# A two-layer streaming block in fp32 on TensorE: a new order for the steps between the q projections and the first merge, and form F7 made by VectorE

## The reference, cut to what matters

```python
h = rms_norm(x, norm_g)
proj = h @ w_in
(q, k, v, z_a, p_in, z_b, u, v_sgu, z_c, glu_a, glu_b, z_d, merge) = jnp.split(proj, SPLIT_POINTS, axis=-1)
q = apply_rope(rms_norm(q.reshape(B, S, N_Q_HEADS, HEAD_DIM), q_norm_g), cos, sin)
k = apply_rope(rms_norm(k.reshape(B, S, N_KV_HEADS, HEAD_DIM), k_norm_g), cos, sin)
o_a = window_attention(q, k, v, attn_sinks)
o_c = spatial_gating(u, v_sgu, sgu_ln_g, sgu_ln_b, sgu_w, sgu_b)
...
branches = jnp.stack([o_a * jax.nn.silu(z_a), o_b * jax.nn.silu(z_b), o_c * jax.nn.silu(z_c), o_d * jax.nn.silu(z_d)], axis=2)
branch_out = jnp.einsum('bsnw,nwd->bsnd', branches, w_branch)
gates = jax.nn.sigmoid(merge.reshape(B, S, N_BRANCHES, D))
return x + jnp.sum(gates * branch_out, axis=2) @ w_out
```

## Time and profile before

| | |
|---|---|
| Time, median of 3 runs | 2082.21 us (2080.82 to 2083.49) |
| Profiled execution, its own time | 2081.95 us |
| Its span, first to last instruction | 2080.2 us |
| Mean granted TensorE clock | 0.994 of full speed |
| Busy: TensorE | 2052.1 us, 99% |
| Busy: VectorE, GpSimd, ScalarE | 1359.6, 1307.6, 906.0 us (65, 63, 44%) |
| HBM | 88 GB/s over the span |
| Chain of work that ended last | TensorE 90%, VectorE 5% |

### The profile page before, as it was taken

The page is one execution under the profiler, slowest core; times in us unless marked ns, Lnnn a source line. Parts: engine busy times, 40 slices in busy tenths (PEclk is TensorE's granted clock), DMA queues, the critical chain, the costliest instruction groups (busy, mean ns, idle before and its releaser), DMA issues.

```text
span 2080.2 us, 27152 instructions
## 1 busy us (share of the span) xinstructions
PE 2052.1 (99%) x9592; PEld 1698.6 (82%) x9592; DVE 1359.6 (65%) x1601; ACT 906.0 (44%) x1679; POOL 1307.6 (63%) x984
## 2 busy tenths in 40 slices
PE   9899999999999999999998999999999999999999
PEld 8788777888888888888887887778888888888887
DVE  6967444688978645338779665447888786453384
ACT  6564565243233434324645546543332333343342
POOL 2666544776669776654738664447767696675545
PEclk9999999999999999999999999999999999999999
DMA  7022332413431343313421232323235313434132
GB/s 273 26 77 75 87 122 72 127 51 72 84 84 51 82 86 76 133 57 111 143 90 36 76 96 88 102 84 104 61 72 95 74 51 82 82 81 137 46 132 102
DMA packets 122214, 186.13 MB, mean 89 GB/s; under 512 B 30688, under 2 KB 39648, under 8 KB 122080
## 3 DMA queue, kind: packets, MB, share of 16 engines
q1 hardware_dynamic: 104496, 155.01, 24.1%
q0 software_dynamic: 9216, 16.78, 6.0%
q10 hardware_dynamic: 8368, 12.60, 1.8%
HBM read 141.34 MB, written 41.95 MB: 88 GB/s over the span
## 4 chain that ended last, share of the span: by engine, by line
PE 90%; DVE 5%; ACT 1%; POOL 1%; issue 1%; DVEq 1%; DMA 0%; SPq 0%; ACTq 0%; POOLq 0%
PE acc L786 81%; PE acc L843 2%; PE aux L843 2%; DVE flo L1601 2%; PE aux L955 1%; DVE x L1605 1%; PE aux L946 1%; PE aux L936 1%; PE aux L904 1%; PE aux L970 1%; POOL wsum L705 1%; DVE stv L1976 0%; PE acc L1010 0%; DMA raw<-wstream 0%; SPq L548 0%
## 5 line engine op out<-in xcount | busy, mean ns | idle before, releaser
L786 PE MATMUL acc<-fhi,whi 128*128 128x512 f32 x2136 | 840.9, 394 | 7.2 <-DVE v L1598 3.0
L786 PE MATMUL acc<-flo,whi 128*128 128x512 f32 x2136 | 835.8, 391 | 0.0
L786 PE MATMUL acc<-fhi,wlo 128*128 128x512 f32 x2136 | 835.6, 391 | 0.0
L701 POOL TENSOR_TENSOR wlo<-raw,whi 128x512 fp32r<-128x512 f32 x392 | 541.9, 1384 | 432.6 <-ACT whi L1062 431.7
L786 PEld LDWEIGHTS acc<-fhi,whi 128*128 128x128 f32 x2136 | 403.5, 189 | 96.9 <-issue 7.7
L786 PEld LDWEIGHTS acc<-fhi,wlo 128*128 128x128 f32 x2136 | 403.1, 189 | 84.3
L786 PEld LDWEIGHTS acc<-flo,whi 128*128 128x128 f32 x2136 | 403.5, 189 | 82.2
L701 POOL TENSOR_TENSOR wlo<-wsum,whi 128x512 fp32r<-128x512 f32 x222 | 315.6, 1422 | 235.3 <-ACT whi L1062 234.8
L1062 ACT ACTIVATE whi<-raw 128x512 fp32r<-128x512 f32 x392 | 244.6, 625 | 342.2 <-PE acc L786 301.1
L1605 DVE SCALAR_TENSOR_TENSOR aux<-conv,allp,aux 128x1024 f32<-128x1024 f32 x232 | 299.0, 1289 | 20.0 <-issue 0.4
L1062 ACT ACTIVATE whi<-wsum 128x512 fp32r<-128x512 f32 x222 | 139.3, 628 | 213.7 <-PE acc L786 139.5
(11 more groups left out here) (236 smaller groups left out, 2286.0 us busy)
## 6 DMA issues: line engine op xcount, KB each, us to landing
raw<-wstream SPq DMA_DIRECT2D x392, 256.0 KB, 2.7
md<-prev POOLq DMA_DIRECT2D x64, 256.0 KB, 4.3
x<-x SPq DMA_DIRECT2D x32, 256.0 KB, 5.2
md<-prev SPq DMA_DIRECT2D x32, 256.0 KB, 3.3
out<-x ACTq DMA_DIRECT2D x32, 256.0 KB, 2.1
mx<-md SPq DMA_DIRECT2D x24, 256.0 KB, 4.9
xrow<-x_rows SPq DMA_DIRECT2D x8, 512.0 KB, 6.8
qs<-qd SPq DMA_DIRECT2D x32, 128.0 KB, 2.7
```

The costliest lines, as they stand in the source:

```text
L701: nc.gpsimd.tensor_tensor(wlo[:, f % SLOTS, :], src, whi[:, f % SLOTS, :].bitcast(F32), ALU.subtract).then_inc(lo_made, 1)
L786: mm = nc.tensor.matmul(dst, w, m[:, kt0 + k, cols], start=first and k == 0 and n == 0, stop=last and k == UK - 1 and n == 2, skip_group_c ...
```

## The change

It does four things, in both layers:

1. **F7 on VectorE.** `form_7` and its semaphore go; `form` makes F7 between the rests of B22 and F6, with two subtractions more on VectorE, and ScalarE's rounding of F7 waits for `form_made`.
2. **Statistics.** VectorE's sixteen `bn_stats` move from between the rests of F5 and F7 to three places: two tiles behind F4, three behind F4's rest, three behind `square_low(L, 0)`. The aggregates, `sgu_var` and the rest of the scales then follow, so that they stand behind `sum_21` of Q0, which waits for Q0's p4. On ScalarE `sgu_scales` and `normal_vs(L, 0)` move from Q0's p3 and p4 to Q1's p6, and `normal_vs(L, 1)` from Q1's p2 to p4. F4's rounding moves behind the weight copy of p5.
3. **Head sums and mix.** On TensorE k's head sums move from ahead of p1 to ahead of p5 of Q1, the first mix from p2 to p3, q's first head sums from p4 of Q1 to ahead of U0. ScalarE's inverse roots, `square_high`, `swap_k` and `load_rope` move with them (`load_rope` from behind the copy of p7 to behind that of p3).
4. **Rotation.** In ZC0 VectorE's table and turn of q's second half move from behind `gate_rest` C22 to behind `sum_22`, and join from behind the whole pair to behind `gate_rest` C22.

```diff
-        MADE = [(q, n) for q in ("F5", "F6", "F4") for n in range(2)]
+        MADE = [(q, n) for q in ("F5", "F7", "F6", "F4") for n in range(2)]
...
-            def form_7(L):
-
-                pool.wait_ge(form_made, form_n(L, MADE, "F5", 1))
-                for n in range(2):
-                    at = slice(2 * n, 2 * n + 2)
-                    nc.gpsimd.tensor_tensor(x12[:, at, :], x22[:, at, :], x12[:, at, :], ALU.subtract).then_inc(f7_made, 1)
-
...
-                form_7(L)
                 row_low(L)
...
-                pair(L, "Q", 1, {"p1": lambda L=L: head_sums(L, 0), "p2": lambda L=L: sgu_mix(L, (0, 1)),
-                                 "p4": lambda L=L: head_sums(L, 1)})
-                pair(L, "U", 0)
+                pair(L, "Q", 1, {"p5": lambda L=L: head_sums(L, 0), "p3": lambda L=L: sgu_mix(L, (0, 1))})
+                pair(L, "U", 0, {"p1": lambda L=L: head_sums(L, 1)})
...
                 plain_pair("Q", 0, first_of(qlo[0]), {
-                    "p1": lambda: take_kv(L, 1), "p6": lambda: form_rounded(L, ("F4", 0), ("F4", 1)),
-                    "p2": lambda: (take_turned_k(L), square_a(L, 0), square_high(L, 0)),
-                    "p3": sgu_scales, "p4": lambda: normal_vs(L, 0, range(TT))})
+                    "p1": lambda: take_kv(L, 1), "p5": lambda: form_rounded(L, ("F4", 0), ("F4", 1)),
+                    "p2": lambda: (take_turned_k(L), square_a(L, 0), square_high(L, 0))})
                 plain_pair("Q", 1, first_of(qlo[1]), {
-                    "p1": lambda: (square_a(L, 1), square_b(L, 1), inverse_root(L, 0)),
-                    "p6": lambda: swap_k(L), "p5": lambda: square_high(L, 1),
-                    "p7": lambda: load_rope(L), "p2": lambda: normal_vs(L, 1, range(TT)),
-                    "p3": lambda: inverse_root(L, 1)})
-                plain_pair("U", 0, None, {"p6": lambda: square_a(L, 2), "p5": lambda: square_b(L, 2)})
+                    "p1": lambda: (square_a(L, 1), square_b(L, 1)),
+                    "p6": lambda: (sgu_scales(), normal_vs(L, 0, range(TT))),
+                    "p5": lambda: inverse_root(L, 0),
+                    "p7": lambda: (square_high(L, 1), swap_k(L)),
+                    "p3": lambda: load_rope(L), "p4": lambda: normal_vs(L, 1, range(TT))})
+                plain_pair("U", 0, None, {"p1": lambda: inverse_root(L, 1), "p6": lambda: square_a(L, 2),
+                                          "p5": lambda: square_b(L, 2)})
...
-                    if q == "F6":
-                        dve.wait_ge(f7_made, 2 * L + n + 1)
                     dve.drain()
                     if q == "F5":
                         op = sub(b11, b11, b12)
+                    elif q == "F7":
+                        op = sub(b12, b22, b12)
...
                 form_rest(L, ("B22", 0), ("B22", 1))
+                form(L, "F7")
                 form(L, "F6")
...
                 form_rest(L, ("F6", 0), ("F6", 1), ("F5", 0), ("F5", 1))
-                dve.wait_ge(vs_taken, 8 * L + 8)
-                gate_stats(range(TT))
                 form_rest(L, ("F7", 0), ("B21", 0), ("F7", 1), ("B21", 1))
                 form(L, "F4")
+                dve.wait_ge(vs_taken, 8 * L + 8)
+                gate_stats(range(2))
                 sum_x(L, "Q", 0)
                 sum_v(L, "Q", 0)
                 sum_22(L, "Q", 0, qhi[0][:, HALF:SEQ])
                 form_rest(L, ("F4", 0), ("F4", 1))
+                gate_stats(range(2, 5))
+                sum_12(L, "Q", 0, qlo[0][:, HALF:SEQ]).then_inc(taken["c"], 1)
+                sum_21(L, "Q", 0, qhi[0][:, 0:HALF]).then_inc(taken["d"], 1)
+                square_low(L, 0)
+                gate_stats(range(5, TT))
+                dve.drain()
                 for t in range(TT):
                     nc.vector.bn_aggr(mv[:, t, :], stv[:, t, :, :])
...
-                sum_12(L, "Q", 0, qlo[0][:, HALF:SEQ]).then_inc(taken["c"], 1)
-                square_low(L, 0)
+                row_bias()
+                sum_x(L, "Q", 1)
                 dve.wait_ge(sgu_root, L + 1)
...
-                sum_21(L, "Q", 0, qhi[0][:, 0:HALF]).then_inc(taken["d"], 1)
-                row_bias()
-
                 add_squares(L, 1)
-                sum_x(L, "Q", 1)
                 sum_v(L, "Q", 1)
+                sum_22(L, "Q", 1, qhi[1][:, HALF:SEQ])
                 square_low(L, 1)
-                sum_22(L, "Q", 1, qhi[1][:, HALF:SEQ])
...
-                gate_pair(L, "ZC", 0, branch_c, 0, 0, {"x": lambda: join(0), "11": lambda: (table(1), turn(1))})
-                join(1)
+                gate_pair(L, "ZC", 0, branch_c, 0, 0, {"x": lambda: join(0), "22": lambda: (table(1), turn(1)),
+                                                       "11": lambda: join(1)})
```

More of the change, by code:

```diff
@@ L326, in hybrid_block @@
         form_made = sem("form_made")
-        f7_made = sem("f7_made")
         form_hi = sem("form_hi")
@@ L1155, in form_rounded @@
                         act.wait_ge(h_scaled, 16 * L + {"B11": 0, "B22": 8, "B21": 12}[q] + 2 * (n + 1))
-                    elif q == "F7":
-                        act.wait_ge(f7_made, 2 * L + n + 1)
                     else:
```

## The result

The changed kernel takes 2063.34 us (median of four runs, 2063.27 to 2063.84); the kernel before, run beside it on the same chip, 2082.43 (2080.82 to 2083.49). The ratio is 0.991, with a 95% interval of 0.9892 to 0.9927: 19.1 us less, nearly twice the forecast 10.2, and 0.7 us under the lower end of the range. The profiled execution spans 2061.5 us against 2080.2, 18.7 less.

The account below looks back on a forecast made before the run. TensorE, busy 99% of the span, bounds the kernel, so only its waits and low clock can be won back: 30.1 us gone less 19.9 new, net 10.2, takes 2081.95 to 2071.8 us; range 2064 to 2079.

Parts of the forecast that it names:

- the gate mix: Ahead of p3 of Q1, both layers: new TensorE wait of 5.6 us plus 3.0 of low clock, 17.2 in all.
- the rotary tables: Loaded later behind the mix, delaying k's rotation: TensorE waits 1.1 us per layer at U0's p4, 2.2 in all.
- Gone, 30.1: Old TensorE waits and low clock removed: head sums 14.1, form 4.5, probabilities 10.1, small ones 1.4 us.
- The probabilities: Waits for normalised probabilities, both layers, go as q's stores and the weight unit behind them come earlier: 10.1 us.
- The head sums' cause: k's squares in Q1 late because ScalarE rounded F4 ahead of p4's copy, which GpSimd's sums awaited; 14.1 us goes.
- S: Start of Q1's p1, when Q0's p4 ends and sum_21 can run; the mix's chain was counted to S + 20.1.
- The 3.0: Low clock charged behind each gate mix wait, in us; bounds 1.7 and 3.4.
- v1, 0.5: First layer: v1 from 1.3 us before to 1.3 after TensorE's p3 asks; 0.5 us charged.
- The mix in time: Rival at the gate mix: no wait, only 3 of the 20 us come, some 2054 to 2056; chance 0.08.
- the probabilities did not wait: Rival at the probabilities: they still wait, 4 to 10 of 10.5 us missing, 2076 to 2082; chance 0.18.
- idle lap of GpSimd: Slower rival: a lap of 4 to 6 us ahead of ScalarE's sqrt delays mix and head sums; chance 0.06.
- the signs that the forecast named: In the new profile: mix waits 5 to 7 us, clock 0.5 to 0.6 behind, 1 us at U0's p4, old waits gone.

Follow-up runs that it names:

- the run alone: Only the second q rotation moved ahead of ZC0's first gates, on the kernel before: 2069.43 us, ratio 0.9944.
- the run with the root first: Kernel after, with k's inverse root on ScalarE ahead of the gate's normalised halves, right behind the sqrt: 2057.27 us, ratio 0.9881.
- the last run: Kernel after with root first, mix one product later, q's six rotation products behind v1's bank work, plus four statistics back between rests of F5 and F7: 2052.08 us.
- rounding moved: Kernel before, with ScalarE's copy for p4 of Q0 put ahead of its rounding of F4: 2079.71 us, ratio 0.9991.
- form alone: Kernel before, with only form F7 moved from GpSimd to VectorE, the sixteen statistics left in place: 2079.58 us, ratio 0.9992.

## Why the prediction was wrong in size and right in kind

All the old waits went, and the one new wait of some length came where the forecast had it. Two terms of the sum failed: the gate mix, charged 17.2 us and measured 12.9, and the rotary tables, charged 2.2 and measured nothing. What the sum called gone was also some 3 us too small; the ledger gives the places of that, and only in part its causes. Point by point, by its own terms.

- **Gone, 30.1.** All of it went. **The probabilities** were forecast at 10.1, or 10.5 with GpSimd's 0.45. The ledger has 11.0 at this place in the changed kernel and in the run alone: waits of 6.7, GpSimd's 0.45 in the second layer, 3.4 of lower clock (7.2 x 0.24 behind each wait), and 0.5 that no wait shows. So this term was about right. The medians' 12.3 alone and 11.9 on top have intervals over 2 us to either side, and the run alone had also less of the lower clock behind the head sums (below), which is no merit of the rotation. **The head sums' cause** was only partly as stated: the rounding made a third to a half of their lateness.
- **New: the mix, 17.2; measured 12.9.** This is the step that failed most. The waits are 5.04 and 4.08, not 5.6 each, which is 2.1 of the 4.3 us; the lower clock is the other 2.2. The chain had two errors that in the first layer partly cancel: the variance came 1.4 us later (sum_21 starts at S + 1.1 instead of 0.3, and the aggregates and the two products with rms take 0.4 longer than charged), and reciprocal to shift took 0.7 instead of 2.5, because its two 128x8 products took 0.96 and 1.16 us in the trace of before only beside GpSimd's pieces; now GpSimd's last piece ends at 106.2, and they take 0.17 each. In the second layer sum_21 starts at S + 0.3 as forecast, the normalisations at S + 9.3, and the wait is 1.0 shorter. The lower clock cost 2.1 and 1.7 where I took 3.0 each. The 3.0 came from the waits of 3.5 and 4.6 in one execution. In the run of the rotation alone the same waits, 3.57 and 4.55 us, are followed by only half of it:

```profile
103.80:111.00 7.20, 7.14 (x24) 5.73 (x25) 3.98 (x9) 4.76 (x10) 3.62 (x3) 0.76 0.24 73
1131.40:1138.60 7.20, 7.17 (x24) 5.75 (x25) 3.95 (x8) 4.79 (x10) 3.59 (x3) 0.76 0.29 73
```

  7.2 x 0.24 = 1.7 in each, against 2.9 and 3.1 in the earlier trace rows. The mix's own price differs as well: with the rotation back, waits of 5.05 and 4.09 us are followed by 7.2 us at 0.65 and 0.66, 2.5 and 2.4 us lost. I had taken a value that differs from one execution to the next for a constant.
- **New: rotary tables, 2.2; measured nothing.** Their issue is as late as forecast, 3.2 us behind the mix's end (125.76; before 0.5), but they land 4.4 us later instead of 7.2: k's rotation starts 1.4 us behind U0's start, forecast 3.9. Its first product took 2.18 us (before 1.28). The two products behind `xs` took 1.23 us each, where the trace of before shows 1.90 and 2.16 beside GpSimd's pieces. Issue by ScalarE's queue, then VectorE:

```profile
125.76 0.44 ACTq L1259 DMA_DIRECT2D sint<-rope  x1
...
130.21 2.18 DVE L1594 SCALAR_TENSOR_TENSOR kraw<-kraw,allp,cost 128x1024 f32<-128x1024 f32 x1 [1.40 <-DMA sint<-rope]
132.31 1.27 DVE L1594 SCALAR_TENSOR_TENSOR kt<-kt,allp,sint 128x1024 f32<-128x1024 f32 x1
...
135.25 1.23 DVE L1587 TENSOR_TENSOR kt<-kt,kraw 128x1024 f32<-128x1024 f32 x1
136.55 1.23 DVE L1584 TENSOR_TENSOR kt<-kt,tmp 128x1024 f32<-128x1024 f32 x1
```

  VectorE even stood 0.89 us idle between the pairs, waiting for TensorE. The mechanism is real all the same: with the mix one product later the wait of 1.4 to 1.8 us is there, at the product that the forecast named, and VectorE works without a pause from the tables' landing (128.08) to the sum that it waits for. Why the tables land faster stays open.
- **New: v1, 0.5; measured nothing for v1** (the 2.3 us for v stand elsewhere), but 0.59 and 0.98 for low halves, which the forecast had not.
- **Order and form together** were forecast at 30.1 - 10.1 - 19.9 = 0.1 us and measure 6.3 (2081.56 to 2075.28); the rotation was 10.1 and measures some 12 by the medians. Of the 8.9 us that the sum was short, the mix is 4.3, the tables 2.2, the probabilities 0.5, less 1.1 for low halves against v1. The ledger places another 2.3: 1.6 between U0 and the scores, where the kernel before had waits of 0.20 and 0.19 at U0's p4 and gaps of 0.5 and 0.2 ahead of the scores that the sum left out, 0.4 at the kernel's start, 0.3 behind the probabilities. The 0.7 left are the medians against the profiled executions (0.4) and 0.3 that I cannot place.
- **The rivals and the signs.** The mix in time did not come, the probabilities did not wait (their margin, forecast at 1 us, is 0.4), and no idle lap of GpSimd fell ahead of the sqrt (it started at 105.00, as soon as the variance was there). The range had bounds for the new terms only, and the 30.1 carried none, though its parts of lower clock were each read once. New waits and clock measure 9.1 + 3.8 + 1.6 = 14.5, so what went is 18.7 + 14.5 = 33.2. A mix near its lower bound, free tables and 3 us more gone all pull one way; only the low halves, 1.1, pull the other. That the terms shared a sign is partly chance, partly perhaps not: how much GpSimd works beside VectorE is in the chain and in k's rotation alike. Of the signs that the forecast named, three were off: the second layer's mix wait is 4.1 us, not 5 to 7, the clock behind the mix 0.7 to 0.8, not 0.5 to 0.6, and U0's p4 does not wait.
- **ScalarE's table loads.** The rows show two loads, 1.28 us each, ahead of Ln and of Exp, in the kernel before, the changed one and the run with the root first. The Trainium skill ("ScalarE: Activation LUTs", Table sets: the hidden batching unit) has one load for the pair; the measurement decides, and the second load is 1.3 us on the chain that the mix waits for. Whether it can be avoided wasn't tried.

## What to carry to other kernels

Price a step by the rows of the same instruction in both conditions, alone and beside the engine that shares its memory: a 0.17 us instruction that costs 1.1 in the row at hand is a statement about its neighbour, and the change may move the neighbour. When a wait is released by a chain over two engines, look in the chain for idle time in the second engine and for independent work behind it in its queue; here turning two entries of ScalarE's order gave 6 us, a third of the whole change again. And where stores and loads share a queue, the place of the last producer of the stores sets when the next loads start: here both came 9 us earlier by two lines, worth two thirds of this change.

## What the runs showed of the hardware that I had not expected

**Not all of VectorE's work slows GpSimd.** Timeline of GpSimd, first before (VectorE makes statistics at that time), then after (it makes the rests of forms, two inputs in SBUF):

```profile
78.13 1.30 POOL L701 TENSOR_TENSOR wlo<-wsum,whi 128x512 fp32r<-128x512 f32 x1
79.56 1.30 POOL L701 TENSOR_TENSOR wlo<-raw,whi 128x512 fp32r<-128x512 f32 x1
```

```profile
78.03 2.27 POOL L700 TENSOR_TENSOR wlo<-wsum,whi 128x512 fp32r<-128x512 f32 x1
80.26 2.27 POOL L700 TENSOR_TENSOR wlo<-raw,whi 128x512 fp32r<-128x512 f32 x1
```

The sixteen statistics between the rests had been 5 us of free passage for GpSimd; with eight rests in a row, and F4 behind them, it gets seven pieces at 2.20 to 2.28, and the two new waits for low halves, 0.59 and 0.98 us, stand there. In the last run the piece beside the four statistics took 1.30 and its neighbours 2.20 and 2.28, and these waits were 0.8 us in all instead of 1.3. The Trainium skill has the rule ("SBUF — State Buffer", Who interferes with whom): an instruction of VectorE with two SBUF inputs contends with GpSimd's reads, one with a single SBUF input outside the two-port modes does not. The trace agrees on both sides; I had used the page only for the sizes of two holds, not for what the moved statistics would uncover.

**The lower clock has no fixed price per wait.** Behind waits of 2.33 and 1.41 us (mix one product later) the clock stayed at 2.4 GHz; behind 2.9 (root first, first layer) 7.2 us ran at a mean of 0.76 (part of it at 1.2 GHz), behind 1.93 (second layer) at 1.00. The length of the wait alone does not decide it: behind 2.94 us (rounding moved, second layer) the clock was 1.00, behind 2.13 (form alone, mix of the second layer) 7.3 us ran at 0.77. Behind 4.6 us it was once 0.57 and once 0.76, with the same instructions. For a wait of that length a single reading tells the cost only to within a factor of two.
